# Where the modulation products are made: moved from the Fourier stage into the late input stage

## The reference, cut to what matters

```python
mod_lat = jax.nn.silu(c) @ w_mod[layer] + b_mod[layer]
sh1, sc1, g1, sh2, sc2, g2 = jnp.split(mod_lat[:, None, :], 6, axis=-1)
prj_l = modulate(rmsnorm(x, norm1[layer]), sh1, sc1) @ w_in[layer]
...
mix_l = jnp.concatenate([y_l, fourier_mixer(f_l, w_four[layer])], axis=-1) @ w_out[layer]
x = x + g1 * mix_l
...
mod = c_act @ w_ada[l] + b_ada[l]
```

## Time and profile before

| | us |
|---|---|
| median of three runs | 3131.88 (3130.84 to 3138.63) |
| span of the profiled execution | 3136.6 |
| end of the input stage (first issue of ssd_scan) | 469.36 |
| Fourier stage, its first issue to that of the next | 700.94 to 821.64 |

### The profile page before, as it was taken

How to read it: one execution, slowest core, us unless ns; L and a number is a source line. 1 busy time by engine, 2 the same in 40 slices (tenths; PEclk the granted TensorE clock), 3 DMA queues, 4 the chain that set the end, 5 groups by cost and what they waited for, 6 DMA issues and landing times. The chain is left out here.

```text
span 3136.6 us, 36957 instructions
## 1 busy us (share of the span) xinstructions
PE 2816.6 (90%) x14094; PEld 1878.9 (60%) x14094; DVE 1226.3 (39%) x1848; ACT 639.7 (20%) x1057; POOL 231.0 (7%) x242
## 2 busy tenths in 40 slices
PE   4999996987798899999998599799888899999998
PEld 2888775762576545445544487687666645445444
DVE  3666317885524311111113564673442611111113
ACT  4322323641302000000002422233120200000002
POOL 0000000000000000000002121121000000000002
PEclk6999997998999899999999699899898899999999
DMA  6642226779735799999996413453653699999995
GB/s 246 242 163 71 74 76 198 222 226 422 269 111 204 286 408 410 409 411 406 412 411 227 114 48 108 81 122 111 228 188 130 273 388 412 409 409 406 409 410 215
DMA packets 294747, 812.65 MB, mean 259 GB/s; under 512 B 38364, under 2 KB 160760, under 8 KB 232432
## 3 DMA queue, kind: packets, MB, share of 16 engines
q1 hardware_dynamic: 248864, 702.45, 60.1%
q10 hardware_dynamic: 30640, 62.81, 5.5%
q0 software_dynamic: 15136, 45.91, 4.2%
HBM read 693.18 MB, written 117.91 MB: 259 GB/s over the span
## 5 line engine op out<-in xcount | busy, mean ns | idle before, releaser
L710 PE MATMUL m_ps_y<-m_wa,m_hTa 128*128 128x512 f32 x560 | 255.5, 599 | 0.0
L689 PE MATMUL m_ps_ga<-m_wa,m_xTa 128*128 128x512 f32 x560 | 253.0, 605 | 1.1 <-issue 1.1
L699 PE MATMUL m_ps_b<-m_wb,m_xTb 128*64 128x256 f32 x2240 | 249.5, 381 | 0.0
L689 PE MATMUL m_ps_ua<-m_wa,m_xTa 128*128 128x512 f32 x560 | 246.0, 592 | 0.0
L1145 PE MATMUL xp_acc<-xp_xh,xp_wh 128*128 128x512 f32 (+3 forms) x600 | 223.0, 372 | 6.7 <-DVE xp_xl L1419 6.7
L1146 PE MATMUL xp_acc<-xp_xl,xp_wh 128*128 128x512 f32 (+3 forms) x600 | 221.2, 369 | 0.0
L1147 PE MATMUL xp_acc<-xp_xh,xp_wl 128*128 128x512 f32 (+3 forms) x600 | 221.1, 368 | 0.0
L699 PEld LDWEIGHTS m_ps_b<-m_wb,m_xTb 128*64 128x64 f32 x2240 | 157.8, 137 | 102.3 <-issue 26.5
L812 DVE TENSOR_TENSOR m_hida<-m_ps_ua,m_sila 128x512 f32<-128x512 f32 x35 | 24.2, 691 | 471.1 <-PE m_ps_ua L689 471.1
L780 ACT ACT_TABLE_LOAD x35 | 44.9, 1283 | 756.3 <-PE m_ps_ga L689 675.7
L2379 PE MATMUL xq_acc<-xq_xh,xq_wh 128*128 128x512 f32 x448 | 180.7, 403 | 13.5 <-DVE xq_xl L2801 8.4
(11 more groups left out here) (553 smaller groups left out, 4455.1 us busy)
## 6 DMA issues: line engine op xcount, KB each, us to landing
m_wa<-in_w_dram SPq DMA_DIRECT2D x102, 1024.0 KB, 11.3
m_wb<-in_w_dram SPq DMA_DIRECT2D x102, 1024.0 KB, 12.0
m_wa<-in_w_eg_dram SPq DMA_DIRECT2D x36, 1024.0 KB, 13.1
m_wa<-in_w_eu_dram SPq DMA_DIRECT2D x36, 1024.0 KB, 11.5
m_wb<-in_w_eg_dram SPq DMA_DIRECT2D x36, 1024.0 KB, 11.2
m_wb<-in_w_eu_dram SPq DMA_DIRECT2D x36, 1024.0 KB, 14.6
m_wa<-in_w_ed_dram SPq DMA_DIRECT2D x36, 1024.0 KB
m_wb<-in_w_ed_dram SPq DMA_DIRECT2D x36, 1024.0 KB, 16.1
```

Of the source, the lines that this page charges most:

```text
L689: last = nc.tensor.matmul(out[:, :], xT_a[:, j, :], w[:, k, :], start=(j == 0), stop=(j == J - 1))
L699: last = nc.tensor.matmul(ps_b[c * SB:(c + 1) * SB, p // 2, :], xT_b[:, j, :], w[:, k, c * HF:(c + 1) * HF], start=(j == 0), stop=(j == J ...
L710: last = nc.tensor.matmul(ps_y[:, d * NF:(d + 1) * NF], hT_a[:, k, :], w[:, c, d * NF:(d + 1) * NF], start=(k == 0), stop=(k == JF - 1))
```

## The change

mod_tiles goes, and with it all that fourier did for it. In mixer1_in the same columns are handled as ten groups c of 1024. SP loads a group's eight slices, 512 KB each, into mring of four slots, behind the weights of chunk n = 21 + c; the ring lies where the convolution's buffers were, so the first load waits until these are free. ScalarE multiplies the first slice by the conditioning value of each partition (mod_first, in its loop 18 + c), VectorE adds the seven others (mod_rest, in its loop 18 + c, behind the low part), PE sums over the partitions with a column of ones (mod_summed, between the halves of chunk 21 + c, the last two behind chunk 28), and VectorE adds the bias (mod_biased, in loop 22 + c and behind the loops). SP loads the biases behind the first group and stores the rows at the very end. step_sizes, sums and decay_values move one loop ahead. M0 is 18, NCH 29, NM2 10. The diff, cut:

```diff
-    R = 5
-    groups = [(k, g) for k, part in enumerate(parts) for g in range(part[1].shape[1] // 512 // NQ4)]
-    steps = [(n, k, g, j) for n, (k, g) in enumerate(groups) for j in range(J)]
...
-    def load(sp):
-        for i, (n, k, g, j) in enumerate(steps):
-            if i >= R:
-                sp.wait_ge(s_mm, i - R + 1)
-            sp.dma_start(ring[:, i % R, :, :].rearrange("p q n -> p (q n)"),
...
-            for q in range(NQ4):
-                act.dma_start(row[q * CG:q * CG + 1, n0:n0 + n, :], b_v[q:q + 1]).then_inc(s_b, 16)
-            n0 += n
-        act.wait_ge(s_c, 16 * len(parts))
...
+    M0 = Z0 + 1
...
+        MC, MR, MA = 1024, 4, 3
+        groups = [(k, g) for k, part in enumerate(mod_parts) for g in range(part[1].shape[1] // MC)]
+        NM2 = len(groups)
...
+        mring, macc, mrow = sb("mring", [P, MR, MC]), sb("macc", [P, MA, MC]), sb("mrow", [P, NM2, MC // NQ4])
...
+        def conv_buffers_free(eng):
+            eng.wait_ge(s_cv, NM)
+            eng.wait_ge(s_xc, NM)
+            eng.wait_ge(s_tq, Q_DT + 1)
+            for r in range(4):
+                eng.wait_ge(s_to[r], 16 * len(range(r, 3 * NT, 4)))
...
+                conv_buffers_free(pool)
+                nc.gpsimd.memset(mrow[:, :, :], 0.0).then_inc(s_mz, 1)
...
+                def mod_weights(c):
+                    k, g = groups[c]
+                    w_m = mod_parts[k][1].rearrange("(p j) n -> p j n", j=J)
+                    if c == 0:
+                        conv_buffers_free(sp)
+                    for j in range(J):
+                        i = J * c + j
+                        if i >= MR:
+                            d, e = divmod(i - MR, J)
+                            if e == 0:
+                                sp.wait_ge(s_m1, d + 1)
+                            else:
+                                sp.wait_ge(s_mf, (J - 1) * d + e)
+                        sp.dma_start(mring[:, i % MR, :], w_m[:, j, g * MC:(g + 1) * MC]).then_inc(s_mw[i % MR], 16)
+
...
+                            sp.dma_start(mrow[q * CG:q * CG + 1, c0:c0 + n_c, :], b_v[q:q + 1]).then_inc(s_mb, 16)
...
+                def mod_store():
...
+                            sp.dma_start(o_v[q], mrow[q * CG:q * CG + 1, c0:c0 + n_c, :]).then_inc(s_ms, 16)
...
+                    if n >= M0 + 3:
+                        mod_weights(n - M0 - 3)
+                    if n == M0 + 3:
+                        mod_biases()
+                for c in range(NCH - M0 - 3, NM2):
+                    mod_weights(c)
...
+                def mod_summed(c):
+                    pe.wait_ge(s_mf, (J - 1) * (c + 1))
+                    if c < 2:
+                        pe.wait_ge(s_te, Q_SUM + 2 + c)
+                    else:
+                        pe.wait_ge(s_me, c - 1)
+                    n = MC // NQ4
+                    for q in range(NQ4):
+                        last = nc.tensor.matmul(mod_sum(c)[q * CG:q * CG + 1, :], ONE[:, 0:1], macc[:, c % MA, q * n:(q + 1) * n],
+                                                start=True, stop=True)
+                    last.then_inc(s_mr, 1)
...
+                        if g == 0 and n >= M0 + 3:
+                            mod_summed(n - M0 - 3)
...
-                    if n == DT + 4:
+                    if n == DT + 3:
...
+                for c in range(NCH - M0 - 3, NM2):
+                    mod_summed(c)
...
+                def mod_first(c):
+                    i = J * c
+                    if c == 0:
+                        act.wait_ge(s_msg, 1)
+                    act.wait_ge(s_mw[i % MR], 16 * (i // MR + 1))
+                    if c >= MA:
+                        act.wait_ge(s_mr, c - MA + 1)
+                    k = groups[c][0]
+                    nc.scalar.activation(macc[:, c % MA, :], mring[:, i % MR, :], ACT.Copy, scale=msg[:, k, 0:1]).then_inc(s_m1, 1)
...
-                        if n == DT + 2:
+                        if n == DT + 1:
                             step_sizes()
-                        if n == DT + 5:
+                        if n == DT + 4:
                             decay_values()
+                        if n >= M0 and n - M0 < NM2:
+                            mod_first(n - M0)
...
+                def mod_rest(c):
+                    k = groups[c][0]
+                    v.wait_ge(s_m1, c + 1)
+                    for j in range(1, J):
+                        i = J * c + j
+                        v.wait_ge(s_mw[i % MR], 16 * (i // MR + 1))
+                        nc.vector.scalar_tensor_tensor(out=macc[:, c % MA, :], in0=mring[:, i % MR, :], scalar=msg[:, k, j:j + 1],
+                                                       in1=macc[:, c % MA, :], op0=ALU.mult, op1=ALU.add).then_inc(s_mf, 1)
+                        v.wait_ge(s_mf, (J - 1) * c + j)
...
+                def mod_biased(c):
+                    if c == 0:
+                        v.wait_ge(s_mb, 16 * NQ4 * len(mod_parts))
+                    v.wait_ge(s_mr, c + 1)
+                    nc.vector.tensor_tensor(mrow[:, c, :], mod_sum(c), mrow[:, c, :], ALU.add).then_inc(s_me, 1)
...
+                    if n >= M0 + 4:
+                        mod_biased(n - M0 - 4)
+                    if n >= M0 and n - M0 < NM2:
+                        mod_rest(n - M0)
+                for c in range(NCH - M0 - 4, NM2):
+                    mod_biased(c)
...
-                mod_load(sp)
-                mod_store(sp)
...
-                    mod_products(pe, t, t + 1)
-                mod_products(pe, T, 3 * T)
...
-                    mod_products(pe, 3 * T + 2 * k2, min(n_mod, 3 * T + 2 * k2 + 2))
...
-                mod_silu(act)
...
-                mod_finish(v, 0)
...
-                mod_finish(v, 1)
```

More of the change, by code:

```diff
@@ L904, in _ @@
                         nc.vector.tensor_tensor(row[r, g, :], acc[r, g, :], row[r, g, :], ALU.add).then_inc(s_row, 1)
-def mod_tiles(nc, ctx, parts, acc):
-    R = 5
-    groups = [(k, g) for k, part in enumerate(parts) for g in range(part[1].shape[1] // 512 // NQ4)]
-    steps = [(n, k, g, j) for n, (k, g) in enumerate(groups) for j in range(J)]
[L914 to L924, removed]
-    def load(sp):
-        for i, (n, k, g, j) in enumerate(steps):
-            if i >= R:
-                sp.wait_ge(s_mm, i - R + 1)
-            sp.dma_start(ring[:, i % R, :, :].rearrange("p q n -> p (q n)"),
[L931 to L938, removed]
-            for q in range(NQ4):
-                sp.dma_start(o_v[q], row[q * CG:q * CG + 1, n0:n0 + n, :]).then_inc(s_out, 16)
-            n0 += n
[L942 to L952, removed]
-                act.dma_start(row[q * CG:q * CG + 1, n0:n0 + n, :], b_v[q:q + 1]).then_inc(s_b, 16)
-            n0 += n
-        act.wait_ge(s_c, 16 * len(parts))
[L956 to L977, removed]
@@ L1042, in mixer1_in, with cb @@
         aT = sb("aT", [3 * H, T, P])
+        MC, MR, MA = 1024, 4, 3
+        groups = [(k, g) for k, part in enumerate(mod_parts) for g in range(part[1].shape[1] // MC)]
+        NM2 = len(groups)
+        mcs, msg = sb("mcs", [P, len(mod_parts), J]), sb("msg", [P, len(mod_parts), J])
+        with ExitStack() as conv_only:
+            def cb(name, shape):
+                return conv_only.enter_context(nc.sbuf_tensor(f"xp_{name}", shape, F32))
+            xpad = cb("xpad", [P, 2, PADW])
+            cacc = cb("cacc", [P, OUTW])
+            xc = cb("xc", [P, 2, OUTW])
+            to = cb("to", [P, 4, 4, P])
+            dtT = cb("dtT", [2 * H, TT * P])
+        mring, macc, mrow = sb("mring", [P, MR, MC]), sb("macc", [P, MA, MC]), sb("mrow", [P, NM2, MC // NQ4])
         xin = bT
@@ L1108, in _ @@
                 sp.dma_start(alog[:, :], a_log.rearrange("d h -> (d h)").partition_broadcast(P)).then_inc(s_din, 16)
+                for k, part in enumerate(mod_parts):
+                    sp.dma_start(mcs[:, k, :], part[0].rearrange("(p j) -> p j", j=J)).then_inc(s_mc, 16)
                 sp.wait_ge(s_zr, 1)
@@ L1118, in _ @@
                     sp.dma_start(a_dram[q].rearrange("c h l -> h c l"), aT[2 * H * q:2 * H * q + H, :, :]).then_inc(s_ad, 16)
-                for r in range(4):
-                    sp.wait_ge(s_to[r], 16 * len(range(r, 3 * NT, 4)))
                 sp.wait_ge(s_ad, 32)
+                mod_store()
             @block.tensor
```

48 lines of the change are left out of this document (28 added, 20 removed).

## The result

| | before | after |
|---|---|---|
| median, us | 3133.91 (3130.84 to 3138.63, 4 runs) | 3149.24 (3144.00 to 3153.07, 4 runs) |
| median, us, second time | 3137.36 (15 runs) | 3149.14 (6 runs) |
| profiled span, us | 3136.6 | 3142.3 |
| input stage, first issue to that of the scan | 439.52 | 482.48 |
| scan | 231.58 | 230.58 |

The changed kernel is slower by 0.4%: ratio 1.0043, 95% interval 1.0031 to 1.0055, and 1.0041 (1.0026 to 1.0056) when timed again. The forecast was 3126.5 in a range of 3108 to 3147, so the time lies above the range. The stages are counted from each stage's first issue on SP's queue to the next one's.

A forecast was written before the change was run, and what follows sets the result against it. The Fourier stage was taken as bound by 41.9 MB of loads and the chain woven with them, the late input stage by PE. Gain 32.2 us, cost 26.8 us: net -5.4, median 3131.9 to 3126.5, range 3108 to 3147.

The forecast's parts named there:

- (a): Fourier stage, eight fo_u steps: without mod products 1.93 us a step instead of 2.90, no first-load wait; gain 7.7 us.
- (b): Fourier stage, VectorE phase: runs back to back and loses two bias additions; gain 1.2 us.
- (c): Fourier stage, rotation phase: eight steps, 4.5 us per two from the third on, 21.4 instead of 36.9; gain 15.5 us.
- (d): End of the Fourier stage: only a hand-over of 0.5 us to the next stage remains; gain 7.8 us.
- Rival C: Fourier rotation phase stays at the slow 1.2 GHz clock, 29.8 instead of 21.4 us; net +3, 3135 us; chance 0.06.
- Rival D: Input stage: loads do not start in loop 17 but a chunk later; +11, net +6, 3138 us; chance 0.04.
- DMA is not near: Late input stage: DMA engine times add to 13.5 us a chunk against PE's old 10.88, so DMA sets the sum.
- Most of it within four loads queued: Input stage: decay_values ahead of the third group takes 5.4 us, mostly covered by queued loads; 1.5 us idle taken.
- The other two idle times: Input stage: full ring awaits ScalarE's first copy, 3.4 us; eight bias loads hold SP 5.2, queue empty about 3.5.
- Rival B: Input stage slower: ring of four halves bound by latency if unqueued landing passes 4.0 us; +18, 3145 us; chance 0.20.
- Rival A: Input stage: weights and stores fill gaps of big loads, PE binds; cost 11, net -21, 3111 us; chance 0.22.
- PE's end: Input stage: PE falls behind DMA's pace, chunk 28 starts at 466, ends at 477 and is not last.

The follow-up runs named there:

- i_rows6: Changed kernel with bias and result rows on GpSimd's queue, two row slots instead of ten, and six ring slots instead of four; input stage 475.8 us.
- i_noW: Changed kernel without the weight loads of chunks 22 to 28, which reuse the weights of chunks 20 and 21; input stage 478.4 us.

## Why the prediction was wrong

**The Fourier stage was right.** Forecast 88, -32.2 us; measured 87.8, -32.9. (a) First phase forecast at 24.34 - 7.7 = 16.6, measured 17.45. In part this is luck: two misses nearly cancel. The clock was at its low level when the steps started (0.50 from 755.17 to 759.00), so the first took 3.8 us as before, now for the clock and no longer for a load; that is 1.9 more than forecast. The seven others take 1.72 instead of 1.93, 1.5 less together; why they are shorter is not shown. (b) 38.0 forecast, 38.03 measured. (c) 21.4 forecast, 20.9 measured, with 4.35 a pair against 4.5. (d) Hand-over 0.5 forecast, 0.3 measured. Rival C is refuted: the first step took 3.8, at the 1.2 GHz level, the later ones 1.9, and the granted clock over the phase is 0.91. Rival D too: the first ring load was issued at 343.6.

**The input stage was wrong by 16 us**, 43.0 against 26.8. Measured from the first copy of group 0 (353.32) the forecast left 140.9 us to the stage's end, and it took 160.1. The three parts of these 19.2 us (the copy itself ended at 354.5, two sooner than forecast):

1. *The pace, 9.7 us.* From the copy of group 3 to that of group 9 the sum by DMA's engine time gives 6 x (9.96 + 1.43) + 4 x 2.09 = 76.7 us, measured 86.45. This is the step that failed: "DMA is not near" and the sum behind it took 421 GB/s, measured with a ring of 5.2 MB, for one of 2.1 MB. With six slots the same loops take 75.97 us, so the sum itself was good for a ring that is deep enough.
2. *From group 0 to 3, 6.6 us, the larger part of it decay_values.* 1.5 us were taken for it. From the copy of group 1 to that of group 2 are 389.57 - 370.05 = 19.5 us, 5.1 more than the later loops' 14.4; i_rows6 shows 17.4 against 12.7, 4.7 more. That is 3.6 over the 1.5. The remaining 3 us are the ring's pace again: three loops at 14.4 instead of 13.5. The lines below show the stop; no run left it out.
3. *The end, 2.9 us.* 23.0 us from the copy of group 9 to the next stage instead of 20.1. Of these, the stretch behind 502.12 took 11.3 us where 1.3 + 1.0 + 7.5 were forecast; the rest is the last group's pace.

The timeline of after around decay_values, VectorE and then ScalarE, and below it a window of the stop:

```profile
382.92 1.28 DVE L1421 SCALAR_TENSOR_TENSOR xp_macc<-xp_mring,xp_msg,xp_macc 128x1024 f32<-128x1024 f32 x1 [0.20 <-DMA xp_mring<-in_w_mod_dram]
386.69 0.33 DVE L1400 TENSOR_SCALAR xp_steps<-xp_steps 128x320 f32<-128x320 f32 x1
390.74 5.25 DVE L1421 SCALAR_TENSOR_TENSOR xp_macc<-xp_mring,xp_msg,xp_macc 128x1024 f32<-128x1024 f32 x4 [3.72 <-ACT xp_macc L1275]
...
387.05 0.47 ACT L1287 ACTIVATE x_lnd<-xp_steps 128x320 f32<-128x320 f32 x1 [8.89 <-DVE xp_steps L1400]
389.57 1.13 ACT L1275 ACTIVATE xp_macc<-xp_mring,xp_msg 128x1024 f32<-128x1024 f32 x1
```

```profile
384.00:392.00 8.00, 5.59 (x21) 3.81 (x22) 4.21 (x7) 4.90 (x6) 0.00 (x0) 0.57 0.50 166
```

ScalarE waited 8.89 us for VectorE's operation of decay_values, which stands behind the last product of group 1, and its first copy of group 2 stands behind its own part. No slot came free from 384.2 to 390.7, and the rate fell to 166 GB/s. "Most of it within four loads queued" was the wrong half-sentence: the loads under way do land during the stop, but none is issued behind them, and by the rate the 8 us moved what 352 GB/s move in 8 x 166 / 352 = 3.8, so 4.2 were lost. The other two idle times were near. SP was held 5.4 us by the eight bias loads (5.2 forecast), and taking them away brought the second group 1.8 us nearer (3.5 forecast).

**Rival B is what happened** in its mechanism, with 3145 us for a measured 3149.24 and +18 in the stage for +16. How close the sizes are is luck: B put the weights' 2.1 us on top of each group, which i_noW does not bear out in the steady loops, had 15.4 us a loop for 14.4, and left the terms 2 and 3 above as they were. It had 0.20, and its threshold was misread. It asked for a landing without queue, and 4.0 us was to decide. The 2.8 us that were taken for it follow from no row: the 2.2 that were left of the weights' landing and the 1.245 of the transfer make 3.4. The shortest landing in after was 3.5 us, below 4.0, so by that test the ring would have kept up. But a ring at work has 5.9 / 1.80 = 3.3 loads under way, and each landed in 5.9; that time stands in the turn. B's sum has it nearly right, (0.33 + 5.9 + 1.28) / 4 = 1.88 against 1.80 measured and its own 1.65. The sign by which B was to be told from the forecast was wrong as well: "over 15 apart at a share well under 1". The groups were 14.4 apart at a share of 1.00, which read alone would have confirmed the forecast. The rate decided: 352 GB/s where "over 380" was written. The limit of the memory that the prediction set aside is not it either, near as 352 comes to it: the same stage reached 400 GB/s with six slots. And the 43.0 us are still under the 45 by which the prediction would have called the whole wrong.

In the argument against A the weights' rate is misread: 0.524 MB in 2.09 us are 251 GB/s, not some 260. Nothing hangs on it.

PE's end was wrong too. Chunk 28 was to end at 477; its last eviction is at 496.56, because the sums of each group stand on PE's queue between the halves of a chunk, and PE waited at them, 20.2 us in all for VectorE's bias additions. The sum of a group needs the bank that the bias addition of the group two before frees, and that addition stands behind the next group's products: the sum of the third group started at 418.50, right behind the first bias addition (417.94), though its own products had ended at 401.84. PE was still not last. Rival A is refuted: it had the groups 11.5 apart.

The Trainium skill, DMA: Bandwidth & Descriptors, fits a transfer with 2.0 us plus bytes over 436 GB/s. It stands in the section "Anatomy of one DMA", not in "Measured", where the prediction put it, and it is for transfers issued by GpSimd; the ring's are issued on SP's queue. As an estimate it gives 3.2 us for 512 KB. The shortest landings here, 3.2 to 3.5, agree; the median under load, 5.9, does not. The Trainium skill's rule under "Measured" on the same page, 1 MiB or more a transfer for 75% of the peak, spoke against the change. The runs bear it out only in a small part: the size alone cost 3 to 4%, the smaller ring 27 to 28% (306 against 421 GB/s, 295 against 409), PE's longer hold of a slot included.

**What stays open.** The stage table explains 10 us of a difference of 12 to 15 between medians. All that lies behind the Fourier stage was left as it was, and took between 2309.5 and 2315.8 us from one profile to the next, so the rest is not told apart from that. What a landing under load is made of is open as well: with a landing of 3.5 us four slots would turn in (0.33 + 3.5 + 1.28) / 4 = 1.28 us a load (an estimate), fast enough for the forecast, and it is not shown what stretched it to 5.9. Rings of more than six slots, and the six-slot ring with the rows left on SP's queue, were not run.

## What to carry to other kernels

A rate measured with one ring can't be carried to another: before summing engine times, work out the new ring's turn from a landing under load, and the rate as the ring's bytes over that turn. The work moved under PE here cost almost nothing as long as PE never waited for it, and gave the stage its own pace once PE did: move the part that fits, in every second loop if need be, and leave the rest where it was. Where the ring is the bottleneck, count a stop of the engines that empty it nearly in full, as with the 5 us of decay_values.

## What the runs showed of the hardware

- Nearly the same DMA share went with different rates: 352 GB/s at 1.00 with the four-slot ring, 334 at 0.95 without the weights, 400 at 1.04 with six slots, and 421 at 1.01 in before's Fourier stage.
- Rate against the size of the ring, in the Fourier stage: 2.1 MB 295 (halves) and 306 GB/s (whole), 3.1 MB 372 (halves), 5.2 MB 409 (halves) and 421 (whole). The rings of 2.1 and 3.1 MB were measured at a granted clock of 0.50, that of 5.2 MB at 0.64 to 0.67.
- Landings grow with the ring: 4.8 us in the median for 1 MB loads with two slots, 10.7 with five; 5.7 for 512 KB loads with four slots, 7.8 with six.
- Loads and stores of 1 KB on GpSimd's queue landed in 3.6 to 5.0 us in the median over the input stage's end, and four took 1.91 us to issue. Chained over a two-slot buffer they made a tail of 23 us.
